# Order of transfers and of the memory rows' preparation in a fused decoder step

## What is computed

```python
def memory_kv(mem, norm_mem, w_ck, w_cv):           # mem: 256 rows of 2048
    hm = rmsnorm(mem, norm_mem)                     # x * rsqrt(mean(x*x) + eps) * gain
    return (hm @ w_ck), (hm @ w_cv)                 # 4 heads of 512

def hybrid_layer(x, mem_k, mem_v, ...):
    h = rmsnorm(x, norm_mix); proj = h @ w_in       # then gated DeltaNet and pooling, 16 channel tiles
    x = x + concat(o_a, o_b) @ w_out
    h2 = rmsnorm(x, norm_cross)
    qx = (h2 @ w_cq)
    scores = einsum(qx, mem_k) * XD ** -0.5         # 4 heads; the 8 requests use cached keys and values
    ctx = einsum(softmax(scores), mem_v)
    x = x + ctx @ w_co
# a final rmsnorm; the memory keys and values are outputs too
```

## Time and profile before

| | us |
|---|---|
| median of 3 runs (lowest, highest) | 1621.17 (1618.49, 1622.15) |
| the profiled execution, its own time | 1621.54 |
| its span | 1619.8 |
| PE busy | 1587.2 (98%) |
| DVE busy, ACT busy | 987.8 (61%), 638.3 (39%) |
| mean granted TensorE clock | 0.995 |
| DMA moved | 274.63 MB, mean 170 GB/s |

### The profile page before, as it was taken

The page is one execution under the profiler, slowest core; times in us unless marked ns, Lnnn a source line. Parts: engine busy times, 40 slices in busy tenths (PEclk is TensorE's granted clock), DMA queues, the critical chain, the costliest instruction groups (busy, mean ns, idle before and its releaser), DMA issues.

```text
span 1619.8 us, 29861 instructions
## 1 busy us (share of the span) xinstructions
PE 1587.2 (98%) x11970; PEld 1434.9 (89%) x11970; DVE 987.8 (61%) x1685; ACT 638.3 (39%) x1094; POOL 154.3 (10%) x170
## 2 busy tenths in 40 slices
PE   6999999999999999999999999999999999799997
PEld 5887899999999999999999999999999998577765
DVE  5676438766867768577345654444598775533455
ACT  5666445442543435434332232223244434422422
POOL 0121000121112111221100001111100000000000
PEclk9999999999999999999999999999999999899999
DMA  7898754332433323323369965888813348978764
GB/s 273 247 290 268 235 140 120 80 95 56 118 94 78 94 66 105 97 75 106 86 163 249 245 171 141 214 212 205 219 45 114 93 125 303 361 252 292 243 248 162
DMA packets 344174, 274.63 MB, mean 170 GB/s; under 512 B 50937, under 2 KB 291458, under 8 KB 343058
## 3 DMA queue, kind: packets, MB, share of 16 engines
q1 hardware_dynamic: 321648, 256.48, 54.2%
q10 hardware_dynamic: 22434, 16.87, 3.8%
HBM read 229.49 MB, written 44.17 MB: 169 GB/s over the span
## 4 chain that ended last, share of the span: by engine, by line
PE 85%; DMA 6%; SPq 4%; DVE 2%; issue 2%; ACT 1%; ACTq 0%; POOL 0%; DVEq 0%; POOLq 0%
PE pj L283 41%; PE pj L504 11%; PE dk L2980 6%; PE pj L2320 4%; PE dk L2320 3%; PE pj L2939 3%; DMA xr<-xT_scratch 2%; PE pj L2947 1%; DMA x_scratch<-xr 1%; PE dk L2602 1%; SPq L2023 1%; DMA w_raw_co<-in_w_co_dram 1%; PE pj L2641 1%; PE dk L1926 1%; PE dk L1303 1%
## 5 line engine op out<-in xcount | busy, mean ns | idle before, releaser
L283 PE MATMUL pj<-a_hi,w_high 128*128 128x272 f32 x1664 | 364.6, 300 | 0.0
L283 PE MATMUL pj<-a_hi,w_low 128*128 128x272 f32 x1664 | 343.4, 288 | 0.0
L283 PE MATMUL pj<-a_lo,w_high 128*128 128x272 f32 x1664 | 343.2, 288 | 0.0
L283 PEld LDWEIGHTS pj<-a_hi,w_high 128*128 128x128 f32 x1664 | 259.3, 189 | 12.4 <-issue 7.9
L283 PEld LDWEIGHTS pj<-a_lo,w_high 128*128 128x128 f32 x1664 | 261.4, 188 | 0.0
L283 PEld LDWEIGHTS pj<-a_hi,w_low 128*128 128x128 f32 x1664 | 260.1, 189 | 0.0
L267 DVE TENSOR_TENSOR w_low<-w_raw,w_high 128x2048 fp32r<-128x2048 f32 x68 | 155.5, 2287 | 83.6 <-ACT w_high L257 83.5
L257 ACT ACTIVATE w_high<-w_raw 128x2048 fp32r<-128x2048 f32 x68 | 130.4, 1918 | 75.7 <-PE pj L283 42.4
L283 PE MATMUL pj<-mix_hi,w_high 128*128 128x272 f32 x512 | 106.2, 288 | 3.1 <-DVE w_low L267 3.1
L283 PE MATMUL pj<-mix_lo,w_high 128*128 128x272 f32 x512 | 105.6, 288 | 0.0
L283 PE MATMUL pj<-mix_hi,w_low 128*128 128x272 f32 x512 | 105.1, 287 | 0.0
(11 more groups left out here) (462 smaller groups left out, 2894.6 us busy)
## 6 DMA issues: line engine op xcount, KB each, us to landing
w_raw<-in_w_in_dram SPq DMA_DIRECT2D x48, 1024.0 KB, 5.9
w_raw_co<-in_w_co_dram SPq DMA_DIRECT2D x28, 1024.0 KB, 7.7
w_raw_wide<-in_w_ck_dram SPq DMA_DIRECT2D x16, 1024.0 KB, 8.6
w_raw_wide<-in_w_cv_dram SPq DMA_DIRECT2D x16, 1024.0 KB, 7.1
w_raw<-in_w_out_dram SPq DMA_DIRECT2D x16, 1024.0 KB, 7.1
keys_s<-keysT_scratch SPq DMA_DIRECT2D x7, 2048.0 KB, 10.2
values_s<-in_cache_mem_v_dram SPq DMA_DIRECT2D x28, 512.0 KB, 8.3
q_part<-in_w_cq_dram SPq DMA_DIRECT2D x48, 256.0 KB, 3.6
```

The source lines that it names most:

```text
L283: mm = pe.matmul(pj[:, 2 * (q % 2) + b, 0:n], wt[:, k, :], x(k, o, n), start=(k == 0 and m == 0), stop=(k == KT - 1 and m == 2))
```

## The change

It has three parts. The buffers' places, the semaphores' counts and the waits that keep them safe are changed along with them.

1. Memory rows: they are turned raw, not scaled. The keys and values that come out are scaled at the copies from PSUM (L600) by the inverted roots, which ACT and DVE now make during the first group (`x_stats` and the new `mem_roots`). `norm_mem` comes first on ACT's queue into a row block of its own and is turned alone; the other gains and the convolution's weights are turned in the third tile. The first weight tile is asked for ahead of the second memory block, the other constants after the second weight tile, `x_prompt`'s block after the sixth. The takes go by both first parts of block 0, then of block 1. `multiply_first` ends the first block (high and low) before the second.
2. Output projection: SP stores the tile before ahead of the late unit; ACT casts the next weight tile ahead of the late unit of the tile before.
3. Attention: the third and fourth weight tiles are asked for ahead of both loads of the second head's keys, whose second half is asked for first; the fourth head's probabilities get a buffer of their own for this. Weight tiles 4 to 7 are asked for at the ends of units 3 to 6, where it was the starts of units 0 to 3.

```diff
@@ sp_mem
             for q in range(3):
                 sp.dma_start(raw_wide[q][:], source("mem", 0, q)).then_inc(w_loaded[q], 16)
                 if q == 0:
+                    sp.dma_start(xin[1][:], t["mem_prompt"][0, P:MEM, :]).then_inc(mem1_loaded, 16)
+                if q == 1:
                     sp.dma_start(cst[:, NFIRST:NCONST], ...).then_inc(ab_loaded, 16)
-            sp.wait_ge(x_scaled, 1)
-            sp.wait_ge(x_loaded, 16)
-            sp.dma_start(xin[0][:], t["x_prompt"][0, 0:P, :]).then_inc(x_loaded, 16)
             for j in range(MEM_GROUPS):
                 for q in range(4):
                     load_ahead(sp, "mem", j, q, j >= KEY_GROUPS)
+                    if j == 0 and q == 2:
+                        sp.wait_ge(squared, 1)
+                        sp.wait_ge(x_turned, 7)
+                        sp.dma_start(xin[0][:], t["x_prompt"][0, 0:P, :]).then_inc(x_loaded, 16)
@@ multiply_first(pe, third, fourth, fifth)
             for m in range(2):
-                pe.wait_ge(x_bank, m + 1)
+                pe.wait_ge(x_bank, (1, 3)[m])
                 for k in range(KW):
                     for x in (hm_hi, hm_lo):
                         pe.matmul(pj[:, m, :], ..., high_wide[0][:, k, :], ...)
-                (second, third)[m](pe)
-            pe.wait_ge(lo_split, 1)
-            for k in range(KW):
-                for m in range(2):
+                if m == 0:
+                    third(pe)
+                    fourth(pe)
+                pe.wait_ge(lo_split, 1)
+                for k in range(KW):
                     mm = pe.matmul(pj[:, m, :], ..., low_wide[0][:, k, :], ...)
+            mm.then_inc(tile_done, 1)
+            fifth(pe)
@@ pe_mem
-            pe.wait_ge(vec_loaded, 16 * 7)
-            pe.transpose(dk[:, 3, 0:NGAIN], ...)
-            pe.transpose(dk[:, 3, P:P + NCONV], ...).then_inc(vec_turned, 1)
+            pe.wait_ge(mem_gain_loaded, 16)
+            pe.transpose(dk[:, 3, 0:KT], vrow[0:KT, 2, :], ident[0:KT, 0:KT]).then_inc(vec_turned, 1)
@@ take_natural
+            if g == 0:
+                eng.wait_ge(inverted, 2)
+            a = eng.tensor_scalar(o, i, over, None, ALU.mult) if m else eng.activation(o, i, ACT.Copy, scale=over)
@@ act_mem
-            x_stats(act, 0, xin[0], P)
-            x_stats(act, 1, xin[1], P)
             take_mem(0)
+            take_mem(1)
             cast_high(act, "mem", 0, 0)
-            take_mem(1)
+            take_mem(2)
+            take_mem(3)
...
+                    if j == 0 and q == 1:
+                        x_stats(act, 0, xin[0], P)
+                    if j == 0 and q == 2:
+                        x_stats(act, 1, xin[1], P)
@@ sp_out
                     sp_residual(sp, j, q)
-                    load_late_units(sp, 4 * j + q, SP_QUARTERS)
                     if q or not is_first(j):
                         sp_x2(sp, 4 * j + q - 1)
+                    load_late_units(sp, 4 * j + q, SP_QUARTERS)
@@ act_out
                     cast_high(act, "out", j, q + 1)
...
+                    if i:
+                        load_late_units(act, i - 1, ACT_QUARTERS)
                     act.wait_ge(pj_read, 80 + i + 1)
                     act.activation(a_hi[...], x2[q % 2][:], ACT.Copy, ...)
                     act.activation(sqx[:], x2[q % 2][:], ACT.Square).then_inc(sqx_ready, 1)
-                    load_late_units(act, i, ACT_QUARTERS)
@@ sp_attention
             load_turned_values(sp, 2)
-            sp.wait_ge(sv_done.sem, sv_done.at(2))
-            load_keys(sp, 1, 0)
             sp.wait_ge(qs_scaled, 1)
             sp.wait_ge(sc_done.sem, sc_done.at(XH))
             load_product(sp, 2)
             load_turned_values(sp, 3)
+            sp.wait_ge(p_turned.sem, p_turned.at(XH - 1))
+            load_product(sp, 3)
             load_keys(sp, 1, 1)
+            sp.wait_ge(sv_done.sem, sv_done.at(2))
+            load_keys(sp, 1, 0)
@@ sp_products
+            sp.wait_ge(p_turned.sem, p_turned.at(XH))
             load_half_rows(sp, 0)
-            sp.wait_ge(p_turned.sem, p_turned.at(XH))
-            load_product(sp, 3)
             for u in range(24):
                 h, step = request_step(u)
-                if u in TILE_UNITS:
+                if u in TILE_UNITS and u >= XH:
                     load_product(sp, TILE_UNITS[u] + 4)
                 if step in (0, 1):
                     sp.wait_ge(sk_done.sem, sk_done.at(2 * h + step + 1))
                     load_values(sp, h, step)
...
+                if 3 <= u < 7:
+                    load_product(sp, u + 1)
```

More of the change, by code:

```diff
@@ L510, in multiply_mem, with multiply_first @@
                         u += 1
-        def multiply_first(pe, second, third, fourth):
+        def multiply_first(pe, third, fourth, fifth):
             pe.wait_ge(hi_cast, 1)
             for m in range(2):
-                pe.wait_ge(x_bank, m + 1)
+                pe.wait_ge(x_bank, (1, 3)[m])
                 for k in range(KW):
@@ L598, in take_natural @@
                 eng.wait_ge(m_turned, 2 * g)
-            o, i = mst[:, m, :], pj[:, 2 * (g % 2) + m, :]
-            a = eng.tensor_copy(o, i) if m else eng.activation(o, i, ACT.Copy)
+            o, i, over = mst[:, m, :], pj[:, 2 * (g % 2) + m, :], mem_over[:, m:m + 1]
+            if g == 0:
+                eng.wait_ge(inverted, 2)
+            a = eng.tensor_scalar(o, i, over, None, ALU.mult) if m else eng.activation(o, i, ACT.Copy, scale=over)
             a.then_inc(pj_read, 2)
@@ L604, in act_mem @@
             act.preload_act_table_set("sqrt_and_others")
+            act.dma_start(vrow[0:KT, 2, :], t["norm_mem"].rearrange("o (k p) -> (o k) p", p=P)).then_inc(mem_gain_loaded, 16)
             for name, o, n in (("norm_mem", G_MEM, 16), ("norm_mix", G_MIX, 16), ("norm_cross", G_CROSS, 16),
@@ L638, in dve_mem, with vectors @@
         def dve_mem(dve):
-            x_scale(dve, 0, xin[0], P)
             dve.wait_ge(vec_turned, 1)
-            dve.tensor_copy(gain[:], dk[:, 3, 0:NGAIN])
-            dve.tensor_copy(convw[:].rearrange("p j g h -> p (j g h)"), dk[:, 3, P:P + NCONV]).then_inc(vec_ready, 1)
+            dve.tensor_copy(gain[:, G_MEM:G_MEM + KT], dk[:, 3, 0:KT]).then_inc(vec_ready, 1)
             dve.wait_ge(vec_ready, 1)
-            x_scale(dve, 1, xin[1], P)
+            def vectors(dve):
+                dve.wait_ge(vec_turned, 2)
+                dve.tensor_copy(gain[:, 0:G_MEM], dk[:, 3, 0:G_MEM])
+                dve.tensor_copy(gain[:, G_MEM + KT:NGAIN], dk[:, 3, G_MEM + KT:NGAIN])
+                dve.tensor_copy(convw[:].rearrange("p j g h -> p (j g h)"), dk[:, 3, P:P + NCONV]).then_inc(vec_ready, 1)
+                dve.wait_ge(vec_ready, 2)
             def take_mem(c):
-                x_take_low(dve, c, c, c // 2, hm_hi, hm_lo, (c % 2) * P, P, G_MEM)
+                block, part = MEM_PARTS[c]
+                x_take_low(dve, c, c, part, hm_hi, hm_lo, block * P, P, G_MEM)
             take_mem(0)
@@ L656, in dve_mem @@
                     split_low(dve, "mem", j, q + 1)
-                    if j == 0 and q == 0:
-                        take_mem(2)
-                        take_mem(3)
+                    if j == 0 and q == 2:
+                        mem_roots(dve, 0)
+                    if j == 0 and q == 3:
+                        mem_roots(dve, 1)
+                        vectors(dve)
                     if j > 0 and q == 0:
@@ L2432, in build @@
         ktb = [take(f"ktb{i}", [DT, MEM]) for i in range(2)]
-        prb = take("prb", [4, MEM])
+        prbs = [take("prb", [4, MEM])] * (XH - 1) + [put("prb_last", [4, MEM], F32, M_B)]
         M_S0, M_S1, M_VW = M_W, M_B + 4096, M_W + 4096
```

71 lines of the change are left out of this document (39 added, 32 removed).

## The result

The changed kernel takes 1631.07 us (median of 5 runs, 1628.39 to 1634.92) against 1621.17 (1618.49 to 1623.07): ratio 1.0063, 95% interval 1.0049 to 1.0078. Measured again on another chip beside its variants it was 1.0044 (1.0026 to 1.0061). So it is slower, by 0.4 to 0.6%; forecast were 1622.7 us and a range from 1611 to 1628. The profiled execution of after took 1628.39 us (span 1626.6), that of before 1621.54: +6.85. Places are read from these two. The profiled one is the fastest of the five of after: of the 9.9 us between the medians the two profiles place 6.85, and where the other 3 lie was not traced.

The account below looks back on a forecast made before the run. PE was taken as the bound, busy 1587.2 of 1619.8 us, so only gaps and half-clock stretches could be won. Start -1.7, output projection -3.1 and last projection +6.3 gave +1.5: 1622.7 us against the median, range 1611 to 1628.

Parts of the forecast that it names:

- The start: Kernel's start: first product at 11.8 instead of 14.51, second tile at 21.3; sum -1.7 us, bounds -2.7 and +1.9.
- `norm_mem` came early, as taken: Start: memory gains land early on ACT's queue, keeping -1.7; landing with the last vector would make it +1.9.
- The output projection: Output projection: earlier residual and cast remove PE's waits for a weight's low part; sum -3.1 us, bounds -3.1 and 0.
- Both waits go: Output projection: PE's two waits for a weight's low part, 3.1 us in all, vanish.
- wanted once a tile: Output projection: the cached keys' load, named next in line, is needed once per tile; PE's tile taken as 11.4 us.
- issued at its old time on SP: Output projection: the cached keys' load keeps its previous issue time on SP's queue.
- The rival that ACT's transfers wait for the cast: Output projection: cached keys come 1.9 us later in each of 14 units; half of it makes +13, 1636 us; chance 0.04.
- The last projection: Last projection: new transfer order moves the wait rather than removing it; sum +6.3 us, bounds 0 and +11.5.
- The two waits: Last projection: PE waits 5.0 us for the first keys, then 9.4 before turning the probabilities, behind the fifth weight tile.
- the forecast's choice to go by the trace: Last projection: 402 GB/s from the trace kept, sum +6.3; the skill's 358 GB/s would make it +7.3.
- The sum: Whole kernel: -1.7 - 3.1 + 6.3 = +1.5 us on 1621.54, so 1623.0; against the median 1622.7.
- The bounds for the output projection: Output projection: from -3.1 us, all that PE waits for, to 0.

Follow-up runs that it names:

- e2: Kernel before with only the output projection's part (store ahead of the late unit, cast ahead of it on ACT): 1.0000 of before.
- e5: The whole change unaltered, run again on one chip with its variants: 1.0044 of before, 1628.64 us.
- e7: Whole change with seven eighths of the bytes of the output projection's late cached keys left out: 1.0013 of before.
- e11: Kernel before with seven eighths of the bytes of the late cached keys left out: 0.9975 of before, 1618.16 us.
- e12: e6 with ACT issuing its half of a late unit ahead of the copy that waits for the residual's add: 0.9904 of before, 1604.72 us.
- e4: Whole change with the last projection's fifth to eighth weight tiles asked for at their units' starts again: 0.9967 of before, 1616.82 us.
- e6: e4 with the second head's first keys ahead of the second half, and half rows behind the fifth weight tile: 0.9924 of before, 1610.97 us.
- e10: Whole change with the second head's first keys ahead of the fourth weight tile and second half, later tiles left late: 1.0031 of before, 1627.05 us.
- e9: e6 with the output projection's cached keys turned on DVE behind the residual's add and its turnings: 1.0169 of before, 1650.35 us.
- e1: Kernel before with only the start's part (raw memory rows, first weight tile ahead of the second block): 0.9994 of before.

## Why the prediction was wrong

**The start** (-1.7 forecast, -1.3 found in the profile). The chain held: first product 11.62 (forecast 11.8), second tile 21.59 (21.3). `norm_mem` came early, as taken; the row of waits now names the constants, 6.2 us. Of the 0.4 us that is missing 0.3 lies in the second tile's start: PE waited 1.03 us for a low part of the second block, until 18.33. By its runs alone the part isn't told from nothing (0.9994).

**The output projection** (-3.1 forecast; nothing won by e2's runs, +2.2 found in after's profile, +0.1 in e5's). This is the step that failed: "Both waits go". I read a chain that ended in PE's wait, store of the old tile, residual, add, cast, split, and took each link as moved by the edit. That reading of before was right, and the links did move: DVE's idle time for the residuals ahead of the adds fell from 25.0 to 13.5 us. But the next link, the load of the cached keys, then held the adds (DVE's idle time ahead of their turning rose from 14.9 to 55.6 us). I had it as "wanted once a tile" and "issued at its old time on SP" without working out its loop, which took 12.9 us against PE's 12.0. Nor did it keep its time on SP: in before it was issued ahead of the add in 7 of 13 tiles (by up to 2.7 us), in after in one. I also had PE's tile as 11.4 us; the traces have 12.00. e7 shows that the new order has no waits once the keys are light, e11 the same for the old one, and e12 that on top of the new order ACT's place alone takes them away with all bytes. What the +2.2 adds to the waits is a stretch at half clock behind the last of them (0.53 over 1176.2 to 1179.6); e5, the same kernel, has none there, so it isn't a price of the change that can be counted on. The rival that ACT's transfers wait for the cast (1636) was wrong: 1093.49 and 1094.06 lie inside the cast of 1093.29 to 1095.19. My reading of that overlap was right: the cast costs the transfers nothing. What I missed is that they do wait for the copy ahead of the cast, so that their place in ACT's list isn't free.

**The last projection** (+6.3 forecast, +5.9 found, of which 4.5 at PE's turn, 4.4 forecast). The two waits, their places and their causes are as described: 3.7 us (forecast 5.0) for the keys at 1394.8, 10.8 (9.4) for the probabilities at 1422.2, led back to the fifth tile's DMA, which landed 9.2 us after its issue as the last of its queue. e4 shows the second by removing it, e6 both. That the sum comes within 0.2 us at PE's turn is in part luck, since two terms miss in opposite directions: the keys landed 20.6 us after the fourth head's scores (forecast 21.9), and from the end of the second request step to the fifth tile's landing it took 11.7 us (forecast 10.2). In that time SP spent 2.4 us in issuing the second values, a term that I had at nothing. In e5 this projection took 8.1 us, inside the bounds of 0 to 11.5. What e10 adds: the two delays do not simply add up, for the late tile's landing is bounded by what lies ahead of it as well as by its issue.

At this step the Trainium skill, "DMA: Bandwidth & Descriptors", section "Where 436 GB/s comes from", puts HBM at about 358 GB/s for a core, as half of what a pair of cores shares. The runs, with one core at work, went above it: between 1390 and 1418 e6 moved 396 GB/s with PE busy throughout, and the earlier trace rows had 402. So the forecast's choice to go by the trace stands.

**The sum.** +1.5 forecast, +6.85 found in the two profiles; 5.3 of the 5.4 us between them is the output projection. By e5's profile it is 3.2, with 1.8 from the last projection. Against the medians the forecast is 8.4 us short (1631.07 against 1622.7), and the 3 us that the profiles don't place stay open. The bounds for the output projection went only from -3.1 to 0: that a reordering could also lose there was left out.

## What to carry to other kernels

Read a stage that repeats as loops, not as one chain: write down for every engine and queue what it stands behind, add up one period of each loop, and compare with the bottleneck's own. Shortening one loop is worth nothing while another stays longer than the bottleneck's period. A queue's transfers stand behind every wait ahead of them in the list, so put them ahead of the instruction that waits for the bottleneck's result, and ask for data in the order of use: here these two moves on top of the change, without a byte less, took the kernel to 1604.7 us, against 1621.0 before, where the change as made cost 0.4 to 0.6%. Moving work to where it looks harmless (e9) can cost 2.5% if a queue with unrelated loads waits for it.

## What the runs showed of the hardware

- DMA issues of ACT's queue ran ahead of the engine's work: in after they were made from 1092.17 on, when the copy ahead of them in the list had just started, and its square and cast, which also stand ahead of them and ended at 1095.19, had not. Until that copy's wait for the add was over (1092.08) none was made, though the keys' turning had ended at 1088.20.
- The time that an issue takes on its queue isn't fixed: that of `xr` between 995 and 1176 us took a median of 0.34 us in before (0.34 to 1.78, 13 of them) and of 2.94 in after (1.66 to 4.32, 13). In after it always comes straight behind the issues of cached keys and of a 1 MB weight tile. In before it took 1.30 and 1.42 where it came straight behind four small stores and a weight tile (1086.32, 1137.04), and 0.34 where the queue had stood still for 2 us (1095.88, 1146.66).
- Waits of PE of 2.50 us (after) and 2.16 (e6) in the output projection were followed by half clock (0.53 over 1176.2 to 1179.6, 0.50 over 1176 to 1180). One of 2.38 us in before was not (1.00 over 1151.4 to 1154.8), nor one of 2.20 in e5, whose kernel is that of after (1.00 over 1174.6 to 1178). e1, which has before's lists there, shows it behind a wait of 2.27 us (0.52 over 1149.7 to 1153.1). So it varies between executions of one kernel; what decides it stays open.
